# Six products of constants on TensorE behind the sums of each norm

## The reference, cut to what matters

```python
def _rms(x, gain, eps=1e-6):
    xf = x.astype(jnp.float32)
    y = xf * lax.rsqrt(jnp.mean(xf * xf, axis=-1, keepdims=True) + eps)
    return (y * gain.astype(jnp.float32)).astype(x.dtype)

def _modulate(h, shift, scale):
    return h * (1 + scale) + shift

def _swiglu(h, w_gate, w_up, w_down):
    return (jax.nn.silu(h @ w_gate) * (h @ w_up)) @ w_down
```

## Time and profile before

| | us |
|---|---|
| median of 3 executions | 2498.3 |
| lowest and highest | 2496.9 and 2502.06 |
| the profiled execution | 2489.76 |
| its span, first to last instruction | 2488.0 |
| TensorE busy | 2310.3 (93%) |
| VectorE busy | 1486.5 (60%) |
| ScalarE busy | 1077.6 (43%) |
| mean granted TensorE clock | 0.976 |

### The profile page before, as it was taken

The page is one execution under the profiler, slowest core; times in us unless marked ns, Lnnn a source line. Parts: engine busy times, 40 slices in busy tenths (PEclk is TensorE's granted clock), DMA queues, the critical chain, the costliest instruction groups (busy, mean ns, idle before and its releaser), DMA issues.

```text
span 2488.0 us, 35474 instructions
## 1 busy us (share of the span) xinstructions
PE 2310.3 (93%) x14882; PEld 1841.4 (74%) x14882; DVE 1486.5 (60%) x2374; ACT 1077.6 (43%) x1824; POOL 135.6 (5%) x174
## 2 busy tenths in 40 slices
PE   6987788999998999998998998989999999998999
PEld 3854356888886777777998863347888888878999
DVE  6337655656565477776555316555666565995454
ACT  4244444322233466665455335554332234435553
POOL 0001200000000000000000002100200100000110
PEclk9998999999999999998999999999999999999999
DMA  7154642444432455444553223432444434444553
GB/s 280 68 203 180 237 171 85 144 143 159 153 127 85 136 170 170 147 158 134 176 190 126 102 72 129 158 136 87 151 156 149 153 110 187 179 150 141 179 195 119
DMA packets 175279, 372.79 MB, mean 150 GB/s; under 512 B 8432, under 2 KB 101872, under 8 KB 160784
## 3 DMA queue, kind: packets, MB, share of 16 engines
q1 hardware_dynamic: 175120, 370.53, 42.8%
HBM read 340.07 MB, written 30.44 MB: 149 GB/s over the span
## 4 chain that ended last, share of the span: by engine, by line
PE 77%; DVE 11%; ACT 7%; issue 2%; DMA 2%; POOL 0%; SPq 0%; DVEq 0%; ACTq 0%; POOLq 0%
PE ps L169 76%; DVE sb_R L200 4%; ACT sb_R L252 2%; DMA sb_slot<-mod_w 1%; PE ps L179 1%; DVE sb_H L200 1%; DVE sb_WP L200 1%; DVE sb_R L229 1%; ACT sb_R L258 1%; ACT L245 1%; DMA sb_slot<-even_w_in 1%; DVE sb_X L217 1%; DVE sb_R L214 1%; DVE sb_X L200 1%; DVE sb_R L217 0%
## 5 line engine op out<-in xcount | busy, mean ns | idle before, releaser
L169 PE MATMUL ps<-sb_HP,sb_WP 128*128 128x512 f32 (+1 forms) x5736 | 1084.0, 350 | 30.8 <-DVE sb_HP L200 26.1
L169 PEld LDWEIGHTS ps<-sb_HP,sb_WP 128*128 128x128 f32 x5736 | 920.1, 191 | 178.4 <-DVE sb_HP L200 24.6
L200 DVE TENSOR_TENSOR sb_WP<-sb_slot,sb_WP 128x1024 fp32r<-128x1024 f32 x380 | 468.8, 1238 | 590.9 <-ACT sb_WP L258 590.5
L258 ACT ACTIVATE sb_WP<-sb_slot 128x1024 fp32r<-128x1024 f32 x380 | 399.3, 1056 | 724.6 <-PE ps L169 710.6
L169 PE MATMUL ps<-sb_XP,sb_WP 128*128 128x256 f32 (+1 forms) x2976 | 498.5, 330 | 0.3 <-DVE sb_XP L200 0.3
L169 PEld LDWEIGHTS ps<-sb_XP,sb_WP 128*128 128x128 f32 x2976 | 446.4, 191 | 51.6 <-DVE sb_XP L200 0.7
L200 DVE TENSOR_TENSOR sb_R<-sb_R 128x256 f32<-128x256 f32 (+4 forms) x411 | 204.4, 533 | 25.0 <-ACT sb_R L252 22.1
L169 PE MATMUL ps<-sb_R 128*32 128x64 f32 (+7 forms) x1768 | 157.6, 285 | 34.2 <-DVE sb_R L200 7.4
L169 PEld LDWEIGHTS ps<-sb_R 128*32 128x32 f32 (+4 forms) x1768 | 112.2, 151 | 85.0 <-issue 44.9
L252 ACT ACTIVATE sb_R<-ps 128x512 f32<-128x512 f32 (+1 forms) x208 | 99.6, 513 | 88.2 <-PE ps L169 84.7
L200 POOL TENSOR_TENSOR sb_R<-sb_R 128x512 f32<-128x512 f32 (+1 forms) x82 | 90.6, 1130 | 827.8 <-ACT sb_R L252 599.3
(11 more groups left out here) (152 smaller groups left out, 1854.7 us busy)
## 6 DMA issues: line engine op xcount, KB each, us to landing
sb_slot<-mlp_w SPq DMA_DIRECT2D x32, 2048.0 KB, 8.7
sb_slot<-mod_w SPq DMA_DIRECT2D x22, 2048.0 KB, 8.7
sb_R<-ada_w SPq DMA_DIRECT2D x12, 2048.0 KB, 7.7
sb_slot<-ada_w SPq DMA_DIRECT2D x24, 1024.0 KB, 4.8
sb_slot<-ffn_w_gate SPq DMA_DIRECT2D x22, 1024.0 KB, 5.5
sb_slot<-ffn_w_up SPq DMA_DIRECT2D x22, 1024.0 KB, 8.1
sb_slot<-ffn_w_down SPq DMA_DIRECT2D x10, 2048.0 KB, 7.7
sb_slot<-odd_w_in SPq DMA_DIRECT2D x32, 512.0 KB, 7.3
```

Of the source, the lines that this page charges most:

```text
L169: return self.e.matmul(out, w, x, start=start, stop=stop, skip_group_check=True)
L200: return BLANK if self.e is None else self.e.tensor_tensor(out, a, b, op)
L258: return self.e.activation(out, a, ACT.Copy) if scale is None else self.e.activation(out, a, ACT.Copy, scale=scale)
```

## The change

A method `warm(bank, n)` makes n products of the identity with the first 256 columns of `cst` into a bank. `Norm.pe` calls it with n = 6 behind the sums, for the bank four places on from the bank of the sums. Hence it comes in all eight stages: in bank 2 for `even`, bank 7 for `ffn1`, bank 4 for the others. The two calls with 0 (ahead of a norm's sums, and in the residual stage `Resid`) make nothing. Nobody reads the results, and the next user of the bank starts it anew.

```diff
+    def warm(self, bank, n):
+        self.vacant(bank)
+        p = self.p
+        for _ in range(n):
+            self.mm(p.ps[bank][:, 0:256], p.c("ident"), p.cst[:, 0:256], True, True)
...
     def pe(self, pe):
         p, a = self.p, self.s0
         pe.vacant(self.bank)
+        if self.WARM[0]:
+            pe.warm(self.bank, self.WARM[0])
         for t in range(1, KT, 2) if self.two else range(KT):
...
         i.then_inc(*pe.sig("sumsq"))
         pe.until(self.bank, "lnsum")
+        if self.WARM[1]:
+            pe.warm((self.bank + 4) % 8, self.WARM[1])
+
+    WARM = 0, 6
...
         pe.vacant(self.bank)
+        if self.WARM:
+            pe.warm(self.bank, self.WARM)
         for g, group in enumerate(self.groups):
...
+    WARM = 0
```

## The result

| | before | with the products |
|---|---|---|
| median of 6 executions | 2496.38 us | 2487.22 us |
| lowest and highest | 2489.83 and 2502.06 | 2481.59 and 2489.13 |
| span of the profiled execution | 2488.0 | 2485.0 |
| mean granted clock | 0.976 | 0.979 |

The ratio is 0.996 with a 95% interval of 0.9941 to 0.9979, or 9.2 us less (5.2 to 14.7). That is faster, beyond the 0.2% named in the prediction. Repeated against 27 executions of the kernel before (median 2495.14), the changed kernel had 2486.11 and a ratio of 0.9961 (0.9946 to 0.9976). The later experiments have executions of the kernel before of their own beside them: median 2495.11 for `transposes`, `twelve`, `two` and `more_warm`, 2496.50 for `transposes24` and `most_warm`.

What follows compares the result with a forecast made beforehand. The prediction took TensorE, busy 93% of the span, as the bound, with time lost to half clock behind waits. Terms -8.31 - 1.10 + 0.8 + 2.77 = -5.8 us from the median 2498.3 gave 2492.5 us, range 2488 to 2501.

Steps and rivals of the forecast that it cites:

- the 0.2% named in the prediction: Whole kernel: a measurement can tell about 0.2%, 5 us, from no change; faster beyond that was given 0.54.
- The mechanism: Six norms' waits for `HP`: products of 2.77 us fit inside, and the clock stays up for the first group.
- The stages' worth: First groups: full clock gains 8.31 us over `ffn0`, `odd`, `mla` and `mlp0`, 1.10 in `mlp1`, 0 in `ffn1`.
- The 0.8 us that I set aside for a fall of the clock in `ffn1`: `ffn1`, wait for the fourth weight piece: lengthened to 2.24 us, it might lose the clock; half of 1.67 us taken.
- `s5` cost: Behind the sums of `s5`: no wait to hide in, so the products add 2.77 us to the path; bounds 0 and 2.77.
- the case of the hidden `s5`: Scan of `s5`: a later wait absorbs the 2.77 us and the clock holds in `ffn1`; 2488.9 us, chance 0.12.
- The sign that I had named: `even`: the first group starts at 42.2 us as before, since a weight transfer sets it; cost 0.
- products of constants do not hold the clock: Six waits: the chip may not count them as work; 2501.1 us, or 2496.4 if half fall; chance 0.20 together.
- Products that outlast the waits: Six waits: at half clock the products take 5.5 us against waits of 3.09 to 4.31; 2511.2 us, chance 0.06.

Runs made afterwards that it cites:

- `transposes`: 12 transposes in place of the six products in each norm but `s5`, against the kernel before: median 2488.12 us, ratio 0.9971.
- `twelve`: Twelve products in place of six in seven norms, none in `s5`, against the kernel before: median 2492.39 us, ratio 0.9981.
- `two`: Two products in place of six in seven norms, none in `s5`, against the kernel before: median 2487.34 us, ratio 0.9976.
- `more_warm`: Six products in seven norms, none in `s5`, plus products ahead of two further waits in `odd`, against the kernel before: median 2479.08 us, ratio 0.9936.
- `transposes24`: 24 transposes in place of the six products in each norm but `s5`, against the kernel before: median 2485.54 us, ratio 0.9948.
- `most_warm`: `more_warm` plus six products ahead of one more wait in `mla`, against the kernel before: median 2477.79 us, ratio 0.9928.
- `before_again`: The kernel before, run and profiled once more unchanged: one execution of 2494.55 us, span 2492.7.
- `no_s5`: The changed kernel without the six products in `s5`, kept in the other seven norms, against the kernel before: median 2485.24 us, ratio 0.9963.

## Why the prediction was partly wrong

**The mechanism held.** Products at 2.75 us (forecast 2.77), hidden in six waits; clock 1.00 in all six first groups; first groups as long after the landmark as before, to 0.02 us (4.22 us in `ffn0` in both). Two products against six showed that the gain comes and goes with the clock of each stage.

**The stages' worth held as a sum, in part by luck.** The means of three traces with the clock falling and two of the changed kernel differ by 2.7 in `ffn0`, 1.0 in `odd`, 2.3 in `mla`, 2.2 in `mlp0` (8.1 against 8.31), and 1.4 in `mlp1` (against 1.10). In `ffn1` 0.15 against 0: there the full clock does little but lengthen the wait for the weight piece. The sum is 9.6 where the forecast had 9.4. Two things offset each other in it. Behind the first groups of `odd` and `mla` the gain over the trace that I had is 1.3 and 1.6 us (forecast 1.40 and 1.70), but over the two other traces with falling clock 2.9 and 2.6: I had sized these terms from one execution. And `odd` gave 1.2 us back some 70 us into the stage, and 0.4 more by its end. At 70 us TensorE waits 3.6 us, and behind that wait the clock stayed at 1.00 in the trace I had the earlier trace rows but not in the changed kernel:

```profile
876.66:884.66 8.00, 8.00 (x39) 0.65 0.00 0
```

Between these two traces `odd` gained nothing (348.3 and 348.5 us). A fall of the clock in another wait of the same stage is a term that the prediction put at nothing. It is not shown to be the change's doing: `before_again` lost the clock there too, for a shorter stretch (0.79 over 8 us).

**Two costs were too high.** The 0.8 us that I set aside for a fall of the clock in `ffn1` did not come; the wait was 1.7 us, not 2.24, because I had left out the small waits on the way, and 1.00 was read behind it. `s5` cost 2.4 to 2.6 us for 2.77 as far as 116 us into the scan, and 2.2 over the whole stage; in the two traces of the changed kernel against the two of before it is 0.9, within that stage's scatter. So the traces make it 9.6 less 0.9 to 2.6, 7.0 to 8.7 us, for the 9.2 (5.2 to 14.7) and 9.0 us timed. The forecast of 5.8 was low by the 0.8 and by 0.2 to 1.9 in `s5`.

**The step that put the time outside the range** was the level: "so I apply the difference to the median: 2498.3 - 5.8". The median of three is not that firm. Over the six executions timed beside the changed kernel the kernel before has 2496.38, 1.9 us lower; over 27 it has 2495.14, 3.2 us lower, and single ones from 2486 to 2503. From 2495.1 the forecast would have been 2489.3, and the case of the hidden `s5` 2485.7. The low end of the range, 2488, stood on that case's number from 2498.3, 2488.9, and left almost nothing for the scatter of the level; the measured 2487.22 lies 0.8 us below. Of the 5.3 us between 2492.5 and the measured median, 1.9 are the level and 3.4 the difference between the kernels. Neither alone would have put the time outside the range; it took both. The timed interval of the difference (5.2 to 14.7) holds the forecast 5.8, so that it was too small is read from the stages, not from the timing. I had the warning in hand: the profiled execution was 8.5 us under the median.

**`even`** cost nothing that can be seen: behind the products TensorE still waits 2.59 us for a transfer. The sum of `start` and `even` is 421.4, 422.7 and 424.6 us in the three traces without products there, and 420.0 to 425.2 in the nine with them; this scatter alone would not exclude a cost of 2 us. The sign that I had named, a first group at 42.2 us, was too sharp: it starts at 40.93 us in the changed kernel, 42.32 in `no_s5` and 42.97 in `before_again`.

**The rivals.** That products of constants do not hold the clock is refuted by the six stretches at 1.00. The rule of the Trainium skill ("TensorE: Matmul & The Clock Gate", Part 4), that transposes do not count as busy in the same way, was not borne out here: 24 transposes of 2.78 us kept 1.00 in the first groups shown and gave the stages of six products. The measurement decides. Products that outlast the waits were made with twelve; at full clock they cost about 3 us in the table and 4.9 behind the first groups, not a loss against before.

What stays open: what besides its length decides whether a wait loses the clock. With 12 transposes `mlp1` was left a wait of 1.77 us and had its old length of 192.66 us; with two products it was left 2.23 us and kept 1.00. So a shorter wait, behind 1.47 us of transposes, lost the clock, and a longer one, behind 1.03 us of products, kept it. Whether short runs of transposes count for less than products, or the moment at which the wait falls decides, no run here separates.

## What to carry to other kernels

Look at the clock behind each wait of TensorE, not only at the wait: in six places half clock behind a wait of 3.1 to 4.3 us cost 9.6 us in all, and idle work placed in the wait, reading constants and writing a bank that nobody reads, gave it back. Put such work only where a wait is there to hide it and TensorE limits what follows; in `s5` it cost nearly its full time, and in `ffn1` it bought next to nothing. Compare stages between landmarks in the trace when a whole execution scatters more than the effect, and single steps inside a stage when the stage scatters too. Size what a fall of the clock costs from several executions: in `odd` one trace showed 1.3 us and two others 2.9. Put the scatter of a median of three into the range.

## What the runs showed of the hardware that was not expected

Transposes of 128x128 in float32 leave one record each and cost half of what I had read from the products: 12 in 1.47 us, 24 in 2.78 us. The 24 kept the clock as six products of the same time did; behind the 12 the clock stayed up in two of six places. A wait of 2.98 us left by two products in `mla` kept 1.00, while one of 3.09 in the earlier trace rows lost it. A wait of 3.58 us that kept the clock in the earlier trace rows was followed by 0.50 in the trace of the kernel without products in `s5` (3.57 us, the stretch from 873.49).
